# RWKV core of a three-block kernel: VectorE's scan over the log decays as two scans of 256 columns, in other slots

## What is computed

```python
w = -jax.nn.softplus(-(w0 + jnp.tanh(xw @ w1) @ w2)) - 0.5
decay = jnp.exp(-jnp.exp(heads(w)))
...
def step(S, inp):
    r_t, w_t, k_t, v_t, kk_t, b_t = inp
    sa = jnp.einsum('bhvk,bhk->bhv', S, -kk_t)
    S = S * w_t[:, :, None, :] + sa[..., None] * b_t[:, :, None, :] + v_t[..., None] * k_t[:, :, None, :]
    return S, jnp.einsum('bhvk,bhk->bhv', S, r_t)
```

## Time and profile before

| | us |
|---|---|
| median of three runs | 1192.62 |
| the three runs | 1192.62, 1189.8, 1196.38 |
| span of the profiled execution | 1187.1 |
| the ten-slot loops of groups 0 to 3 in it | about 91 to 210 |

### The profile page before, as it was taken

The page is one execution under the profiler, slowest core; times in us unless marked ns, Lnnn a source line. Parts: engine busy times, 40 slices in busy tenths (PEclk is TensorE's granted clock), DMA queues, the critical chain, the costliest instruction groups (busy, mean ns, idle before and its releaser), DMA issues.

```text
span 1187.1 us, 24912 instructions
## 1 busy us (share of the span) xinstructions
PE 1147.3 (97%) x10626; PEld 1045.2 (88%) x10626; DVE 746.0 (63%) x1081; ACT 620.5 (52%) x906; POOL 107.6 (9%) x87
## 2 busy tenths in 40 slices
PE   6999989999999999999999999999999999999997
PEld 6798777779999989987999999899997898999996
DVE  7888775375544467896655444768486555655554
ACT  8974653354344345664733433665555564544443
POOL 0032263501100000220010000000000000000000
PEclk9999999999999999999999999999999999999999
DMA  8521111046544644423555446254433442655640
GB/s 303 216 107 65 36 56 56 10 156 234 188 168 187 248 177 157 164 110 140 178 213 182 180 170 250 105 212 178 178 117 133 141 179 91 241 179 182 212 177 36
DMA packets 29805, 187.32 MB, mean 158 GB/s; under 512 B 3472, under 2 KB 5648, under 8 KB 8592
## 3 DMA queue, kind: packets, MB, share of 16 engines
q1 hardware_dynamic: 27072, 177.21, 40.6%
q10 hardware_dynamic: 2640, 8.75, 2.3%
HBM read 184.90 MB, written 1.05 MB: 157 GB/s over the span
## 4 chain that ended last, share of the span: by engine, by line
PE 81%; DVE 11%; ACT 5%; issue 2%; DMA 1%; POOL 1%; ACTq 0%; DVEq 0%; SPq 0%; POOLq 0%
PE ps L2087 24%; PE ps L2088 23%; PE ps L2089 23%; DVE w_lo L1364 2%; PE ps L2220 1%; PE ps L2405 1%; PE ps L2550 1%; PE ps L2410 1%; ACT mixed L631 1%; DVE w_lo L1360 1%; PE ps L2353 1%; PE ps L2792 1%; PE ps L2800 1%; DVE x_tm L1613 1%; PE ps L2407 1%
## 5 line engine op out<-in xcount | busy, mean ns | idle before, releaser
L1364 DVE TENSOR_TENSOR w_lo<-w_raw,w_hi 128x2048 fp32r<-128x2048 f32 x149 | 345.9, 2338 | 133.9 <-ACT w_hi L602 133.4
L2087 PE MATMUL ps<-x_hi,w_hi 128*128 128x256 f32 x1344 | 378.2, 281 | 4.3 <-DVE x_lo L1651 2.4
L2088 PE MATMUL ps<-x_lo,w_hi 128*128 128x256 f32 x1344 | 375.0, 279 | 0.0
L2089 PE MATMUL ps<-x_hi,w_lo 128*128 128x256 f32 x1344 | 374.9, 279 | 0.0
L602 ACT CAST w_hi<-w_raw 128x2048 fp32r<-128x2048 f32 x148 | 281.8, 1907 | 150.5 <-PE ps L2089 149.1
L2087 PEld LDWEIGHTS ps<-x_hi,w_hi 128*128 128x128 f32 x1344 | 252.6, 188 | 10.7 <-issue 5.6
L2088 PEld LDWEIGHTS ps<-x_lo,w_hi 128*128 128x128 f32 x1344 | 252.8, 188 | 1.3
L2089 PEld LDWEIGHTS ps<-x_hi,w_lo 128*128 128x128 f32 x1344 | 252.7, 188 | 0.0
L2087 PE MATMUL ps<-w_hi,hid_hi 128*128 128x512 f32 x304 | 118.7, 391 | 0.1
L2088 PE MATMUL ps<-w_lo,hid_hi 128*128 128x512 f32 x304 | 118.7, 390 | 0.0
L2089 PE MATMUL ps<-w_hi,hid_lo 128*128 128x512 f32 x304 | 118.3, 389 | 0.0
(11 more groups left out here) (399 smaller groups left out, 1770.0 us busy)
## 6 DMA issues: line engine op xcount, KB each, us to landing
w_raw<-in_weights SPq DMA_DIRECT2D x163, 1024.0 KB, 4.8
xt<-in_xT SPq DMA_DIRECT2D x2, 512.0 KB, 5.4
w_raw<-in_weights SPq DMA_DIRECT2D x2, 512.0 KB, 6.2
x_tm<-in_x SPq DMA_DIRECT2D x1, 1024.0 KB, 4.7
gain<-in_mix_g ACTq DMA_DIRECT2D x2, 512.0 KB, 3.8
gain<-in_mix_b ACTq DMA_DIRECT2D x2, 512.0 KB, 5.4
gain<-in_ffn_g ACTq DMA_DIRECT2D x2, 512.0 KB, 6.9
gain<-in_ffn_b ACTq DMA_DIRECT2D x2, 512.0 KB, 8.0
```

Of the source, the lines that this page charges most:

```text
L1364: V.tensor_tensor(w_lo[:, i % WS, :], w_raw[:, i % RAW, :], w_hi[:, i % WS, :].bitcast(F32), ALU.subtract).then_inc(lo_done, 1)
L2087: nc.tensor.matmul(out, hi_l, hi_r, start=start, stop=False)
L2088: nc.tensor.matmul(out, hi_l, lo_r, start=False, stop=False)
L2089: return nc.tensor.matmul(out, lo_l, hi_r, start=False, stop=stop)
```

## The change

`decays` takes a half m and scans the two blocks of feature tile m (256 columns). `cum_ready` now counts halves, and `growth` waits for both. The two halves of group 0 stay together ahead of the loops. Those of group 1 stand in slots 0 and 1 of group 0, those of group 2 in slots 5 and 9 of group 0, and those of group 3 in slots 7 and 8 of group 1. Within a slot they stand behind the sets taken from PE and ahead of `modified_k`, `a_tilde`, `y_mean` and `y_variance`.

```diff
+        SUM_HALVES = {(0, 0): (1, 0), (0, 1): (1, 1), (0, 5): (2, 0), (0, 9): (2, 1), (1, 7): (3, 0), (1, 8): (3, 1)}
...
             def growth(g):
 
-                act.wait_ge(cum_ready, g + 1)
+                act.wait_ge(cum_ready, 2 * g + 2)
...
-            def decays(g):
-
-                k4 = slice(4 * g, 4 * g + 4)
+            def decays(g, m):
+
                 dve.wait_ge(rate_taken, 2 * g + 1)
                 if g:
                     dve.wait_ge(exp_done, g)
                 else:
                     dve.wait_ge(mix_lo_done, 4)
-                V.tensor_tensor_scan(flat(cum), rc("reset"), flat(sw[:, k4, :]), 0.0, ALU.mult, ALU.add).then_inc(cum_ready, 1)
+                V.tensor_tensor_scan(flat(cum[:, 2 * m:2 * m + 2, :]), rc("reset", 0, 2 * P),
+                                     flat(sw[:, 4 * g + 2 * m:4 * g + 2 * m + 2, :]), 0.0, ALU.mult, ALU.add)\
+                 .then_inc(cum_ready, 1)
...
-            decays(0)
+            for m in range(2):
+                decays(0, m)
...
+                    if (g, slot) in SUM_HALVES:
+                        decays(*SUM_HALVES[g, slot])
                     if g < 3:
-                        if slot == 0:
-                            decays(g + 1)
-                        elif slot == 1:
+                        if slot == 1:
                             modified_k(g + 1)
                         elif slot == 4:
                             a_tilde(g + 1)
```

## The result

Before 1192.38 us (median of 20 runs, 1189.51 to 1196.38), after 1194.55 us (20 runs, 1193.05 to 1197.65). The ratio is 1.0024, with a 95% interval of 1.0016 to 1.0032: 2.9 us slower by the ratio, 2.2 by the medians. The forecast was 1196.0, 3.4 us slower. The profiled execution has a span of 1192.0 us, 4.9 more than that of before. The distance between the two differences (2.9 and 4.9) is part of what the experiments explain.

A forecast was written before the change was run, and what follows sets the result against it. The prediction took PE's stream as the bound, TensorE being busy in 97% of the span. Its terms, +2.2 + 0.6 + 1.1 - 0.5, gave +3.4 us and a median of 1196.0, range 1191.0 to 1199.5.

The forecast's parts named there:

- Group 1's late half: Slots 0 and 1 of group 0: growth(1) waits, ScalarE's copies come late, PE stalls in slot 3; +2.2 us.
- Group 2's halves: Slots 5 and 9 of group 0: the half of slot 5 delays VectorE's w_m, for which PE waits; +0.6 us.
- The half of slot 9 and the removed scan of slot 0 of group 1: Groups 0 and 1: half falls where VectorE was idle, cost 0; removed scan gives nothing, as L1526 still waits for PE.
- Group 3's halves: Slots 7 and 8 of group 1: halves beside POOL's instructions make yvar and take_scores late; +1.1 us.
- The other reading in the prediction: Slots 7 and 8 of group 1: POOL stretches a scan by 1.9 rather than holding it back; term 0.9, sum 3.2.
- Slot 0 of group 2: The whole scan of 2.30 us leaves VectorE, but little reaches PE; gain 0.5 us, bounds 0.65 and 0.
- The lower end of the forecast's bounds: Whole loops: -1.7 us, from terms of 0, 0.57 and 0 with 2.3 off.
- rival B: PE's clock also falls behind slot 3 of group 0 and slots 8, 9 of group 1; 1199.4 us, chance 0.12.
- one of the prediction's own signs of being wrong: PEclk falling inside the loops; also no PE wait in slot 3, or group 0's loops under 2 us longer.
- C: PE doesn't wait for ScalarE's copies in slot 3, and group 2's slot 0 scan comes off whole; 1190.9 us, chance 0.08.
- D: Later waits for VectorE shrink and catch up the slot 3 stall; about +1.2, 1193.8 us, chance 0.13.
- E: exp_done or rate_taken binds the moved halves, which run where the whole scans did; about 1192.6 us, chance 0.02.

The follow-up runs named there:

- the pair at (2, 0): Changed kernel with only group 1's halves moved, so both halves of group 3 stand together in slot 0 of group 2; ratio 1.0045.

## Why the prediction was right, and where its terms were off

**Group 1's late half, +2.2:** measured 2.27 at slot 3 (2.20 against the chain's 100.44, from which the forecast counted; stall 2.21), three times with the change or its part. The reading was that of one queue: `mid_plus` idle 0.37 in the earlier trace rows said that ScalarE already waited for the scan, and 100.44 without a pause in the earlier trace rows, against the copy's end at 99.75, said that PE had only half a microsecond of slack. The experiments with `growth` behind the copies and with extra casts show both links apart.

**Group 2's halves, +0.6:** 0.58 at slot 7, by itself and in the whole. The half of slot 9 and the removed scan of slot 0 of group 1 cost and gave nothing, as said.

**Group 3's halves, +1.1:** 0.7. Mis-sized. The way in which it happens is the one forecast: a half that is issued beside a POOL instruction ends one own length behind it (L1287 ends at 151.69 + 1.05 = 152.74, and 0.6 more is 153.34; the half ended at 153.28). The step that failed is that POOL's L1288 was to start only behind the first half. It started at 152.81, beside it, and so ended at 154.11 already; the second half ended at 154.66 by its duration, about 0.6 behind that. So the second half had less left to wait for than I gave it. The other reading in the prediction, a scan stretched by 1.9, would make both halves 1.15 us; they took 1.10 and 0.81.

**Slot 0 of group 2, -0.5, bound -0.65:** VectorE gained 0.85 and PE 0.79 at the state's product. The term is mis-sized, and the bound of 0.65 failed: it took the wait of the earlier trace rows for all that PE could win there. The likely reason is that PE's pair of products ahead of it had waited a little for VectorE too; no run takes that apart. The prediction also took a gain there as kept to the end. It isn't: 0.5 of it is lost again by `yvar` of group 2, so 0.35 is left.

Over the whole of the loops at one clock it is 4.45 - 1.42 = 3.0 us, against a forecast of 3.4 and 2.9 by the ratio. What is too much in the forecast is the 0.4 of group 3's halves. That the gain's term comes near to what is kept (0.5 against 0.35) is luck: it was 0.85 at first, and the loss behind it lies in slots that the prediction doesn't look at. The lower end of the forecast's bounds was also made more loosely than its terms: it took 0 for group 3's halves, whose own bound was 0.4, and 2.3 for a gain bounded at 0.65.

**The clock, rival B at 0.12:** in the profile it came true in part, and PEclk falling inside the loops was one of the prediction's own signs of being wrong. The fall behind the stall is in every execution with the long stall, 3.42 us and 1.42 us of loss in the first profile, where 1.7 were given as price. It didn't decide, since one stretch isn't two, and since the kernel before has such stretches as well, only in other places. The mean granted clock is 0.9953 over the 20 runs of the changed kernel, and 0.9955 over the 86 runs of the kernel before that were taken beside the experiments on three chips (for the 20 runs of it beside the result the clock isn't known). The profiled execution of before, at 0.997, has one whole stretch, that at 211.7; most of its runs, at 0.996, have about two. This fits times that moved by 2.9 us where the spans moved by 4.9, but it isn't shown run by run. On average the kernels with the stall do have more half clock: over the 44 runs of the four measurements with the long stall the mean clock is 0.9946, over the 79 runs of those with no stall in slot 3 it is 0.9962.

My argument against B, that full work on both sides of the stall keeps the clock, was wrong for this place. The trace of the kernel before did have a wait of 2.19 us in full work, at 898.32, with the clock at 1.00 behind it. The prediction didn't look there; it would have spoken against B. So whether the clock falls isn't settled by the kernel alone: it did so behind long waits four times of four in slot 3 and 6 times of 14 near 900 us, and also 2.6 us behind the wait of 0.74 us of slot 7 in the kernel with the cast moved, and behind group 3 with no wait over 0.6 us in the 15 us before it. The sentence of the Trainium skill that was weighed there ("TensorE: Matmul & The Clock Gate", "What's actually happening": an idle PE is put to half rate, a busy one to full) agrees with the stretches behind the long stall. By itself it doesn't place the stretch behind group 3.

**Rivals C and D** fell: PE does wait in slot 3 for ScalarE's copies, and nothing further on takes the stall back. **E** fell: no moved half waits for `exp_done`.

## What to carry to other kernels

This is one kernel and one change. Before an instruction is moved to a later slot, look at who waits for it and then at what stands behind that waiter on its own queue: here 0.6 us of VectorE's work, moved by 3 us, made ScalarE's copies late, and PE lost 2.2 us to a step that has nothing to do with the sums. A move to an earlier slot is cheap only if the engine has a gap there and no POOL instruction on SBUF runs beside it; split in two and put next to POOL, a scan waits twice. A stall in a stream that is otherwise full can have a second price in the clock behind it: here 1.4 us in each of four executions with 2.2 or 2.3 us of stall in slot 3, and none directly behind stalls of 1.2 us. Part of that is paid elsewhere in runs without it, and only timed runs show what is left.

## What the runs showed that I hadn't expected

**Half clock comes in stretches of one length, and their number differs from run to run of the same kernel.** Each stretch that ends inside the span is 3.40 to 3.42 us long in these profiles. The runs of the kernel before fall in steps by their mean granted clock: 11 runs at 0.999 have a median of 1189.2 us, 53 at 0.996 1191.4, 6 at 0.993 1193.6 and 12 at 0.991 1194.7; four lie between. So the scatter of this kernel (1188 to 1195) goes with the number of such stretches. One stretch takes 0.0014 off the mean clock (3.42 / 2 / 1190), so from 0.999 to 0.996 it is about two, and they cost 2.3 us: 1.1 each by this estimate, less than the 1.42 in group 0, where PE is full. For the changed kernel, 13 runs at 0.996 have 1194.1 and 4 at 0.993 1196.9: 2.7 and 3.2 us more than before at the same clock. That is an estimate of the cost of the change without the clock, across chips and occasions, and fits the 3.0 of the landmarks. What makes the clock fall behind a wait in one execution and keep behind the same wait in another stays open; no run here changes it on purpose.

**VectorE and POOL hold each other up by whole instructions** when both read SBUF, as the whole scan, the halves and the pair at (2, 0) show: 1.22 us alone, 2.30 beside one POOL instruction, 3.38 for two halves beside two. The sentence of the Trainium skill in the prediction ("SBUF — State Buffer", "Who interferes with whom") says so for one instruction, and the two halves agree: they take 1.77 us beside L1298 and the rest beside L1299. That a split pays the wait twice was not foreseen.
